# Attention rounds of a transformer kernel: the order of a pair's value products and the next pair's first transposes

## The chip, the cores and the metric

The kernel runs on one core of a Trainium2 chip, in one launch. The metric is the device time of one execution in microseconds (us). The median before the change is 3055.33 us, of two runs (3054.82 and 3055.84).

## The reference, cut to what matters

Two transformer layers and one recurrent and sparse-attention layer are computed for 512 tokens of width 1024, all in float32. Most of the work is matrix products; each kind of attention stands between an input projection and an output projection. What the change touches are the inner rounds of three attentions: layer 0 (`even_mixer`: 8 heads of banded attention with sinks, then 8 heads of stick-breaking attention), layer 1 (`odd_mixer`: 16 heads of dilated attention, computed here as one causal softmax with a table as bias) and the third layer (16 heads of attention over chosen keys).

```python
s = einsum('bnqhgd,bnkhd->bnhgqk', qb, kb) * (dh ** -0.5)
s = where(valid, s + bias, -inf)
p = exp(s - m);  denom = sum(p) (+ exp(sink - m))
o = einsum('bnhgqk,bnkhd->bnqhgd', p / denom, vb)
...
# stick breaking
a = where(strict, exp(log_sigmoid(z) + log_after), 0.0)
o = einsum('bhqk,bkhd->bqhd', a, v)
```

The order of the products is free as far as the reference goes.

## The kernel before, in words

All engine programs are written out by hand, one ordered list of instructions for each engine, with waits on named flags. There is no scheduler: the order in which the functions issue is the order on the engine.

**The three stages.** `Stage` (L1089) describes a run of rounds, one round for each pair of heads. `EV` (L2038) has eight rounds: four pairs of banded heads (`EA`, two groups of rows in a round: rows 2 and 3, rows 1 and 0) and four pairs of stick-breaking heads (`EB`, three groups: row 3, rows 2 and 0, row 1). `OC` (L2158) and `SX` (L2537) have eight rounds each, all with the three groups. Names in the trace begin with `ev`, `oc` and `sx`. A "row" i is a tile of 128 queries against the keys that it may see, so row 3 of a causal pair is 128x512. `u` is the head within the pair.

**A round on TensorE** is written in `pe_stage` (L1165), in the loop of L1246. For the pair g:
- `turn(g, 0, first group)` transposes the first group of head 0's weights (L1201; transposes are at L97). It waits until the bank is drained and until the row is scaled (`normed`, L1209).
- `scores(g + 1, n)` makes the scores of the next pair (L1181), in three places of the round, or two where the next pair has two groups.
- `fill(g, part)` issues matrix products of the projections that stand ahead of or behind the attention (L1169). The number in a round is the stage's `quota`; a table splits it over five places.
- the other `turn`s transpose the remaining groups of head 0 and those of head 1; the last group of head 1 comes just ahead of `fill(g, 3)` or `fill(g, 4)`.
- `values(g)` multiplies the transposed weights with the values (L1215). It waits until every transposed group of the pair has been copied out of PSUM.

Transposes and values share a ring of two PSUM banks (`tbank` and `vbank`, L1129 to L1133). The place in the ring is worked out from the pair and the group alone. The first transposes of pair g + 1 take the bank that the last transposes of pair g held, and the values of g take the other.

**A round on ScalarE** is in `act_stage` (L1273, loop at L1324): `upper(g - 1)` rounds the output of the pair before (it waits for `valued`), then the copy of the first transposed group, `exps(g, 1)`, the other copies with the splitting of projection weights between them (`act_split`), and at the end `copies(g, 1, last)` and then `exps(g + 1, 0)`: the exponentials of head 0 of the next pair. For stick-breaking pairs `sigmoids(g + 1, n)` take the place of the exponentials.

**A round on VectorE** is in `dve_stage` (L1363, loop at L1425): `end(g, 0)`, `lower(g - 1)`, the maxima of group 0 of the next pair, `end(g, 1)`, the other maxima, the weight splitting. `end` is `divide` (L1386: it waits for the exponentials of that head, takes the reciprocals, and scales row 3 first, then rows 2, 0 and 1, each giving `normed`) or `breaks` (L1400: a scan and a product for each row, after GpSimd's masks). `lower(g - 1)` waits for the values of the pair before and for ScalarE's upper half, and frees their bank.

The loop on TensorE before the change:

```python
for g in range(T_.N):
    turn(g, 0, slice(0, 1))
    scores(g + 1, 0)
    fill(g, 0)
    ...
    fill(g, 4)
    values(g)
```

Of the kernel before, what the change touches and what calls it, by code (L numbers as in the profile page):

```python
# [267 lines left out]
def program(nc, T, out):  # L268
# [109 lines left out]
    def handover(e, key):  # L378

        leave(e, key)  # L380
        if e.name != "pe":
            enter(e, key)
# [782 lines left out]
    def pe_stage(pe, T_, before, after, hand):  # L1165
        tag = T_.tag
        count = [0]

        def fill(g, part):  # L1169

            n = T_.quota[g]

            share = (0, 0.16, 0.5, 0.68, 0.86, 1) if g == T_.N - 1 else (0, 0.2, 0.4, 0.6, 0.8, 1)
            if T_.causal and 0 <= g < T_.N - 1:

                share = (0, 0.15, 0.35, 0.55, 0.7, 1)
            for _ in range(int(n * share[part + 1] + 1e-6) - int(n * share[part] + 1e-6)):
                next(before if count[0] < 96 else after)
                count[0] += 1

        def scores(g, n):  # L1181
            if g == T_.N or n >= len(T_.seq[g][0].groups):
                return
            A, s = T_.seq[g]
            kb = A.kv_of(s)
            pe.wait_ge(put, A.qkey(s))
            pe.wait_ge(put, A.kkey(kb))
            group = A.groups[n]
            for u in range(2):
                b = T_.sbanks[u]  # L1190
                pe.wait_ge(drained, pe.held[b])
                pe.held[b] = (tag, g, "s", n, u)
            for both in zip(T_.scores(g, n, 0), T_.scores(g, n, 1)):
                for u, (i, W, dst) in enumerate(both):
                    k0, k1, _, _ = A.spans[i]
                    r = slice(64 * u, 64 * u + 64)
                    ins = pe.matmul(dst, A.qT[r, s, i * P:(i + 1) * P], A.kT[r, kb, k0 * P:k1 * P], start=True, stop=True)
                    if i == group[-1]:
                        ins.then_inc(scored, (tag, g, n, u))

        def turn(g, u, part):  # L1201
            A, _ = T_.seq[g]
            for n in range(len(A.groups))[part]:
                group = A.groups[n]
                b, at = T_.tbank(g, u, n), 0
                pe.wait_ge(drained, pe.held[b])
                pe.held[b] = (tag, g, "t", n, u)
                for i in group:
                    pe.wait_ge(normed, (tag, g, u, i))  # L1209
                    for j in range(A.spans[i][3] // P):  # L1210
                        ins = pe.transpose(bank[b][:, at:at + P], T_.row(g, u, i)[:, j * P:(j + 1) * P], ident)
                        at += P
                ins.then_inc(turned, (tag, g, n, u))

        def values(g):  # L1215
            A, s = T_.seq[g]
            v = T_.vbank(g)
            o_ = bank[v]
            pe.wait_ge(drained, pe.held[v])
            pe.held[v] = (tag, "o", g)  # L1220
            for key in A.vkeys(s):
                pe.wait_ge(put, key)
            for u in range(2):
                for n in range(len(A.groups)):
                    pe.wait_ge(put, (tag, g, n, u))
            if A.total == CAUSAL_W:
                for kt in range(NT):
                    for u in range(2):
                        ins = pe.matmul(o_[64 * u:64 * u + 64, kt * P:S], A.V(2 * s + u, kt), T_.pt[u][:, kt, kt * P:S],
                                        start=kt == 0, stop=kt == NT - 1)  # L1230
            else:
                for i, (k0, k1, o, W) in enumerate(A.spans):
                    for kt in range(k0, k1):
                        for u in range(2):
                            ins = pe.matmul(o_[64 * u:64 * u + 64, i * P:(i + 1) * P], A.V(2 * s + u, kt),
                                            T_.pt[u][:, kt, i * P:(i + 1) * P], start=kt == k0, stop=kt == k1 - 1)
            ins.then_inc(valued, (tag, g))

        for _ in range(96 * T_.last):
            next(before)  # L1240
        for n in range(3):
            scores(0, n)
            fill(-1, n)
        fill(-1, 3)
        fill(-1, 4)
        for g in range(T_.N):  # L1246
            turn(g, 0, slice(0, 1))
            scores(g + 1, 0)
            fill(g, 0)
            turn(g, 0, slice(1, None))  # L1250
            fill(g, 1)
            scores(g + 1, 1)
            if g + 1 < T_.N:
                turn(g, 1, slice(0, -1))
                fill(g, 2)
            else:
                turn(g, 1, slice(0, 1))
                fill(g, 2)
                turn(g, 1, slice(1, -1))
            scores(g + 1, 2)  # L1260
            if g + 1 == T_.N or len(T_.seq[g + 1][0].groups) == 3:
                fill(g, 3)
                turn(g, 1, slice(-1, None))
            else:
                turn(g, 1, slice(-1, None))
                fill(g, 3)
            fill(g, 4)
            values(g)
        handover(pe, hand)
        for _ in after:  # L1270
            pass
# [1853 lines left out]
    def pe_program(pe):  # L3125
        pe.held = {}
        for l, C in enumerate(crosses):
            f1, f2 = ffns[f"f1{l}"], ffns[f"f2{l}"]
            if l:
                handover(pe, f1.up)  # L3130
                pe_gemm(pe, f1.up, {"h": hT(f1.up)}, rates_side(pe_rates, pe, f1.up))
            else:
                pe_f1u0(pe)
            pe_gemm(pe, f1.down, {"f": f1.F})
            handover(pe, "odd" if l else "even")
            pe_stage(pe, OC if l else EV, (pe_in1 if l else pe_in0)(pe), pe_out(pe, C), C.kv)
            pe_kv(pe, C)
            pe_xq(pe, C)
            pe_cross(pe, C)
            pe_gemm(pe, f"xo{l}", {"h": hT(f"xo{l}")})  # L3140
            handover(pe, f2.up)
            pe_gemm(pe, f2.up, {"h": hT(f2.up)}, rates_side(pe_rates, pe, f2.up))
            pe_gemm(pe, f2.down, {"f": f2.F})
# [3 lines left out]
        pe_rnn(pe)  # L3147
        pe_ya(pe)
        pe_stage(pe, SX, pe_products(pe, "gb", {"h": hT("idx2")}), pe_products(pe, "yb", {"h": hT("yb")}), "yb")
        pe_gemm(pe, "wo", {"y": Z})  # L3150
        pe_post(pe)
# [196 lines left out]
```

## Time and profile before

| | |
|---|---|
| median of two runs | 3055.33 us |
| the profiled execution | 3054.1 us |
| its span in the trace | 3052.4 us (1.7 us lie around it) |
| TensorE busy | 3037.4 us of the span |
| VectorE, ScalarE, GpSimd busy | 2036.1, 1416.4, 450.5 us |
| granted TensorE clock over the span | 0.999 of full |
| the rounds of EV, OC, SX in the span | about 447 to 537, 1555 to 1648, 2524 to 2617 us |

Times in timelines are counted from the span's start. Matmuls overlap, and their ends are modelled, so the time of a step on TensorE is best read from the start of one line to the start of the next.

### The profile page before, as it was taken

To read this page: it belongs to the slowest core of one execution; us is meant where nothing else is said; L and a number is where in the kernel's file an instruction comes from. 1 tells how busy PE (TensorE), PEld (TensorE's weight loads), DVE (VectorE), ACT (ScalarE), POOL (GpSimd) and SP (SyncE) were. 2 spreads that over 40 slices of the span, in tenths; PEclk is the share of its full clock that TensorE was granted. 3 is DMA by queue.
4 is the path that set the end of the run, shared out by engine and by line. 5 is a ranking of instruction groups with operands and counts; after the bars stand their busy time and mean duration, and the time that the engine had idled before them with its cause. 6 is when DMAs were issued, how large, how long until landed. Compare 5 with 4: busy or idle time off the path is not lost.

```text
span 3052.4 us, 44801 instructions
## 1 busy us (share of the span) xinstructions
PE 3037.4 (100%) x17960; PEld 2620.2 (86%) x17960; DVE 2036.1 (67%) x2896; ACT 1416.4 (46%) x2189; POOL 450.5 (15%) x550
## 2 busy tenths in 40 slices
PE   9999999999999999999999999999999999999999
PEld 8998886887999899988867879998887786789987
DVE  7886258755888478863565657886336876578873
ACT  5444247544444244442455545444236727454442
POOL 1112014212110021100310212110153200031100
PEclk9999999999999999999999999999999999999999
DMA  7762330423874267633232416763332231247732
GB/s 209 176 165 98 103 97 29 148 67 99 198 176 136 97 160 176 166 107 104 83 99 75 152 49 165 177 167 106 89 96 83 82 105 35 76 111 190 170 117 70
DMA packets 287360, 366.93 MB, mean 120 GB/s; under 512 B 12304, under 2 KB 211344, under 8 KB 287024
## 3 DMA queue, kind: packets, MB, share of 16 engines
q1 hardware_dynamic: 233392, 304.42, 31.5%
q0 software_dynamic: 53184, 59.32, 12.0%
q8 instruction: 142, 2.33, 0.3%
q14 instruction: 66, 0.54, 0.1%
q10 hardware_dynamic: 576, 0.33, 0.0%
HBM read 361.92 MB, written 2.10 MB: 119 GB/s over the span
## 4 chain that ended last, share of the span: by engine, by line
PE 94%; issue 3%; DVE 2%; POOL 1%; ACT 0%; DMA 0%; POOLq 0%; ACTq 0%; DVEq 0%
PE ps L94 91%; PE ps L97 3%; POOL evQ L142 1%; DVE wl L103 0%; POOL evPb L142 0%; POOL evPa L142 0%; DVE hTl L109 0%; DMA misc<-in_misc 0%; DVE xT L103 0%; DVE u_X2l L103 0%; DVE u_raw L103 0%; DVE u_X3l L103 0%; DVE u_X4l L103 0%; DVE evQ L115 0%; DVE s_gb L103 0%
## 5 line engine op out<-in xcount | busy, mean ns | idle before, releaser
L103 DVE TENSOR_TENSOR wl<-raw,wh 128x1024 fp32r<-128x1024 f32 (+2 forms) x485 | 597.0, 1237 | 499.1 <-ACT wh L100 494.9
L100 ACT ACTIVATE wh<-raw 128x1024 fp32r<-128x1024 f32 (+2 forms) x485 | 505.1, 1049 | 810.9 <-PE ps L94 770.0
L94 PE MATMUL ps<-hTh,wh 128*128 128x256 f32 (+1 forms) x2016 | 671.0, 333 | 0.7 <-ACT hTh L100 0.7
L94 PE MATMUL ps<-hTh,wl 128*128 128x256 f32 (+1 forms) x2016 | 666.6, 331 | 0.0
L94 PE MATMUL ps<-hTl,wh 128*128 128x256 f32 (+1 forms) x2016 | 624.0, 330 | 0.2 <-DVE hTl L109 0.2
L94 PEld LDWEIGHTS ps<-hTh,wh 128*128 128x128 f32 x2016 | 383.9, 190 | 42.1 <-issue 9.2
L94 PEld LDWEIGHTS ps<-hTh,wl 128*128 128x128 f32 x2016 | 383.7, 190 | 37.7 <-issue 7.1
L94 PEld LDWEIGHTS ps<-hTl,wh 128*128 128x128 f32 x2016 | 382.1, 190 | 37.4 <-issue 4.7
L100 ACT ACTIVATE wh<-u_raw 128x1024 fp32r<-128x1024 f32 x190 | 201.4, 1062 | 297.8 <-PE ps L94 281.9
L94 PE MATMUL ps<-u_Fh,wl 128*128 128x512 f32 x704 | 273.9, 389 | 0.0
L94 PE MATMUL ps<-u_Fh,wh 128*128 128x512 f32 x704 | 273.9, 389 | 0.0
L103 DVE TENSOR_TENSOR wl<-u_raw,wh 128x1024 fp32r<-128x1024 f32 x190 | 232.2, 1222 | 40.1 <-ACT wh L100 39.7
L103 POOL TENSOR_TENSOR xn<-xn 128x512 f32<-128x512 f32 x69 | 100.1, 1450 | 988.8 <-ACT xn L100 751.4
L94 PE MATMUL ps<-u_Fl,wh 128*128 128x512 f32 x704 | 232.9, 389 | 0.0
L94 PE MATMUL ps<-wh,hTh 128*128 128x512 f32 (+2 forms) x576 | 216.8, 377 | 0.0
L94 PE MATMUL ps<-wl,hTh 128*128 128x512 f32 (+2 forms) x576 | 215.1, 374 | 0.0
L94 PE MATMUL ps<-wh,hTl 128*128 128x512 f32 (+2 forms) x576 | 195.1, 374 | 0.0
L94 PEld LDWEIGHTS ps<-u_Fl,wh 128*128 128x128 f32 x704 | 132.1, 188 | 27.5
L94 PEld LDWEIGHTS ps<-u_Fh,wl 128*128 128x128 f32 x704 | 132.2, 188 | 27.3
L94 PEld LDWEIGHTS ps<-u_Fh,wh 128*128 128x128 f32 x704 | 132.1, 188 | 27.3
L94 PEld LDWEIGHTS ps<-wh,hTh 128*128 128x128 f32 x576 | 108.3, 188 | 20.1 <-issue 2.2
L94 PEld LDWEIGHTS ps<-wl,hTh 128*128 128x128 f32 x576 | 108.4, 188 | 19.2 <-issue 1.4
(423 smaller groups left out, 6106.6 us busy)
## 6 DMA issues: line engine op xcount, KB each, us to landing
raw<-in_ffn_w_gu SPq DMA_DIRECT2D x118, 512.0 KB, 4.6
raw<-in_ffn_w_down SPq DMA_DIRECT2D x88, 512.0 KB, 3.6
u_raw<-in_ffn_w_gu SPq DMA_DIRECT2D x77, 512.0 KB, 4.9
raw<-in_ffn_w_gu POOLq DMA_DIRECT2D x40, 512.0 KB, 6.1
u_raw<-in_ffn_w_gu POOLq DMA_DIRECT2D x38, 512.0 KB, 6.1
raw<-in_xa_w_kv SPq DMA_DIRECT2D x32, 512.0 KB, 3.6
raw<-in_w_in SPq DMA_DIRECT2D x28, 512.0 KB, 3.6
raw<-in_od_w_in SPq DMA_DIRECT2D x24, 512.0 KB, 3.8
```

Of the source, the lines that this page charges most:

```text
L94: return self.made(lambda e: e.matmul(*a, **k))
L97: return self.made(lambda e: e.transpose(*a, **k))
L100: return self.made(lambda e: e.activation(*a, **k))
L103: return self.made(lambda e: e.tensor_tensor(*a, **k))
L142: return self.made(lambda e: e.affine_select(*a, **k))
```

## The change

The call that issues the first transposes of head 0 moves from the top of the round to the end of the round before, ahead of `values`. Round 0 keeps its own at the top. The same instructions are issued with the same operands and banks; no other engine's program is touched.

```diff
@@ -1244,7 +1244,8 @@
         fill(-1, 3)
         fill(-1, 4)
         for g in range(T_.N):
-            turn(g, 0, slice(0, 1))
+            if not g:
+                turn(g, 0, slice(0, 1))
             scores(g + 1, 0)
             fill(g, 0)
             turn(g, 0, slice(1, None))
@@ -1265,6 +1266,8 @@
                 turn(g, 1, slice(-1, None))
                 fill(g, 3)
             fill(g, 4)
+            if g + 1 < T_.N:
+                turn(g + 1, 0, slice(0, 1))
             values(g)
         handover(pe, hand)
         for _ in after:
```

## Rows read from the trace of the kernel before

**Rows 1.** The page: busy time by engine, and the chain that ended last.
```profile
PE 3037.4 (100%) x17960; PEld 2620.2 (86%) x17960; DVE 2036.1 (67%) x2896; ACT 1416.4 (46%) x2189; POOL 450.5 (15%) x550
...
PE 94%; issue 3%; DVE 2%; POOL 1%; ACT 0%; DMA 0%; POOLq 0%; ACTq 0%; DVEq 0%
```

**Rows 2.** Timeline of TensorE, one round of OC (start, us, instruction, count).
```profile
1571.76 0.65 PE L97 MATMUL ps<-misc,ocPa 128*128 128x128 f32 x4
...
1574.98 0.38 PE L97 MATMUL ps<-misc,ocPb 128*128 128x128 f32 x2
...
1576.44 2.38 PE L94 MATMUL ps<-ocPT,o_v 128*64 128x512 f32 x16
1578.75 0.66 PE L97 MATMUL ps<-misc,ocPa 128*128 128x128 f32 x4
1579.33 1.13 PE L94 MATMUL ps<-o_kT,o_qT 64*128 64x512 f32 x4
```

**Rows 3.** Timeline of ScalarE, the same round (in brackets: idle before, releaser).
```profile
1575.39 0.38 ACT L100 ACTIVATE ocPT<-ps 128x256 f32<-128x256 f32 x1 [1.79 <-PE ps L97]
1575.67 0.39 ACT L100 ACTIVATE ocPb<-ocPb,ocsm 128x128 f32<-128x128 f32 x1
...
1578.86 0.60 ACT L100 ACTIVATE hTh<-ps 128x512 fp32r<-128x512 f32 x1 [0.90 <-PE ps L94]
```

**Rows 4.** Timeline of VectorE, the same round.
```profile
1570.75 0.49 DVE L106 TENSOR_SCALAR ocPa<-ocPa,ocsm 128x512 f32<-128x512 f32 x1
...
1577.99 0.18 DVE L124 RECIPROCAL ocsm<-ocsm 128x4 f32<-128x4 f32 x1 [1.43 <-ACT ocPa L100]
1578.20 0.49 DVE L106 TENSOR_SCALAR ocPa<-ocPa,ocsm 128x512 f32<-128x512 f32 x1
...
1579.56 0.69 DVE L103 TENSOR_TENSOR hTl<-ps,hTh 128x512 fp32r<-128x512 f32 x1
```

**Rows 5.** Timelines of TensorE and VectorE, a late round of OC.
```profile
1623.65 2.37 PE L94 MATMUL ps<-ocPT,o_v 128*64 128x512 f32 x16
...
1625.16 0.49 DVE L106 TENSOR_SCALAR ocPa<-ocPa,ocsm 128x512 f32<-128x512 f32 x1
```

**Rows 6.** Timelines of TensorE and VectorE, an early round of SX.
```profile
2545.34 2.37 PE L94 MATMUL ps<-sxPT,s_v 128*64 128x512 f32 x16
...
2547.10 0.49 DVE L106 TENSOR_SCALAR sxPa<-sxPa,sxsm 128x512 f32<-128x512 f32 x1
```

**Rows 7.** Timelines of TensorE and VectorE, first and third banded round of EV.
```profile
456.10 1.75 PE L94 MATMUL ps<-evPT,e_tk 128*64 128x128 f32 x28
...
457.16 0.36 DVE L106 TENSOR_SCALAR evPb<-evPb,evsm 128x256 f32<-128x256 f32 x1
...
477.55 1.75 PE L94 MATMUL ps<-evPT,e_tk 128*64 128x128 f32 x28
...
479.05 0.35 DVE L106 TENSOR_SCALAR evPb<-evPb,evsm 128x256 f32<-128x256 f32 x1
```

**Rows 8.** Timelines of TensorE and VectorE, a stick-breaking round of EV.
```profile
502.84 2.38 PE L94 MATMUL ps<-evPT,e_vb 128*64 128x512 f32 x16
...
501.06 0.69 DVE L103 TENSOR_TENSOR evPa<-evPa,evQ 128x512 f32<-128x512 f32 x1
...
505.96 0.69 DVE L103 TENSOR_TENSOR hTl<-ps,hTh 128x512 fp32r<-128x512 f32 x1
```

**Rows 9.** Waits of TensorE: in total us, times, longest us.
```profile
PE ps L94 <- ACT evQ L100: 3.7, 3, 2.2
```

**Rows 10.** Stretches of EV: length, each engine's busy us, granted clock, DMA.
```profile
482.60:484.86 2.26, 0.09 (x2) 0.04 (x1) 0.29 (x2) 2.26 (x7) 0.63 (x3) 1.00 0.00 0
484.86:486.20 1.34, 1.34 (x8) 0.92 (x8) 0.01 (x1) 1.23 (x3) 0.46 (x2) 0.75 0.00 0
486.20:488.00 1.80, 1.80 (x8) 1.57 (x7) 1.80 (x2) 1.72 (x5) 0.67 (x1) 0.50 0.00 0
488.00:489.00 1.00, 1.00 (x4) 0.41 (x4) 0.97 (x2) 1.00 (x4) 1.00 (x2) 0.53 0.61 35
```

## The prediction

> **What bounds the kernel now.** I read the page first, then TensorE's waits, then the timelines of TensorE, ScalarE and VectorE over the same round. The page shows TensorE busy for 3037.4 of 3052.4 us and on 94% of the chain that ended last [rows 1]. So a microsecond in which TensorE stands still is a microsecond of the kernel, and one on another engine costs nothing until TensorE has to wait for it. The longest kind of wait inside the rounds is 3.7 us in three pieces [rows 9], in the stick-breaking rounds. In OC and SX TensorE waits for nothing that counts. What the change does must therefore be read from one question: when TensorE reaches the moved transposes at their new place, is their input there?
>
> **Softmax rounds of three groups (OC and SX).** Follow the end of a round of OC. TensorE issues the last transposes of head 1 at 1574.98, then some filling products, the values at 1576.44, the first transposes of the next pair at 1578.75 and its scores at 1579.33 [rows 2]. ScalarE had waited 1.79 us for those last transposes; it copies them at 1575.39 and only then begins the next pair's exponentials, at 1575.67 [rows 3]. They take until VectorE, after 1.43 us of idling for them, starts the reciprocal at 1577.99; the 128x512 row is scaled from 1578.20 for 0.49, so it is there at 1578.69 [rows 4]. TensorE takes it at 1578.75. The values (2.31 us from start to start) are the cover of this chain, to within 0.06 us.
>
> The change takes the cover away. After the filling products TensorE reaches the moved transposes at 1576.44 and stands until 1578.69: 2.25 us. The values then queue behind the waiting transposes although their own input is there, and behind them everything on TensorE: the scores, the filling, the next transposes. Nothing of the chain can begin earlier in exchange, because it starts with ScalarE's copy of transposes that stand ahead of the wait, and from that copy to the scaled row it takes the same 3.3 us as before. So the wait isn't earned back in the next round, where the chain starts from a transposition that is as late as the round is.
>
> There are seven such boundaries in each stage (the round 0 transposes are not moved). The first four of OC show 2.24 to 2.25 us in this way. In the last three there is one filling product more, and the row is scaled at 1625.65 against values at 1623.65: 2.00 us [rows 5]. Sum 4 x 2.25 + 3 x 2.0 = 15.0 us. SX shows the same pattern at its seven (2547.59 against 2545.34 is 2.25 us [rows 6], the last three 2.0): 15.0 us.
>
> **Banded rounds (EV, pairs 0 to 3).** The first group begins with row 2. It is scaled at 457.52, the values began at 456.10: 1.42 us; the second boundary is the same; at the third VectorE first drains projection results, and the row comes at 479.40 against 477.55: 1.85 us [rows 7]. Sum 4.7 us.
>
> **Stick-breaking rounds (EV, four boundaries from pair 3 to 7).** Here the input is early: the product that makes row 3 ends at 501.75 and the values begin at 502.84 [rows 8]. The transposes pass without a wait. What is late next is the other side: the values end about 0.6 us later (the transposes take 0.58, 1578.75 to 1579.33 [rows 2]), and ScalarE's upper half (0.60 [rows 3]) and VectorE's lower half wait for them. The lower half, at 505.96 [rows 8], would start near 506.4, and VectorE's scans are queued behind it. VectorE and GpSimd are near their limit in these rounds. Ends: nothing, if their small gaps take it up, or the 0.45 us in each of four. I take 0.25 each, 1.0 us.
>
> **The same shift in the softmax rounds.** ScalarE's upper half starts 0.5 us later with regard to the scores. Head 1's row 3 is ready at 1571.24 and TensorE wants it at 1571.76 [rows 2, 4]: 0.52 us of room. It just goes; ends 0 and 0.1 us in each of 14 rounds, I take 0.
>
> **Handing over.** A row that TensorE now stands for costs the time from VectorE's end to its first transposition as well. I take the 0.06 us seen between 1578.69 and 1578.75 [rows 2, 4], for 17 boundaries 1.0 us. The filling products, copies, buffers and DMAs keep their order; the bank of the moved transposes is drained by the very copy that the values need, so no new wait stands there.
>
> Sum of the waits: 15.0 + 15.0 + 4.7 + 1.0 + 1.0 = 36.7 us.
>
> **The clock.** In EV there is a wait like the new ones: TensorE did nothing for some 2.2 us of 482.60 to 484.86. The granted clock was 1.00 through it and then 0.75, 0.50 (which is the 1.2 GHz level) and 0.53 in the next three stretches [rows 10]. What was lost is 0.25 x 1.34 + 0.5 x 1.80 + 0.47 x 1.00 = 1.7 us. The change makes 17 waits, 14 of them of 2.0 to 2.3 us and three of 1.4 to 1.9. One row can't say whether each such wait brings the clock down: the fall came after the wait, not in it, so how the wait lies seems to matter. Ends: no fall (0 us) and one at each (29 us). The nearest row fell, but three of the waits are clearly shorter and six more a little. I take half of them, 8 x 1.7 = 13.6 us.
>
> In the Trainium skill, "TensorE: Matmul & The Clock Gate", section "HAM oscillation — how this bites in real kernels", a kernel is described whose wait in every tile brought the clock down every time. By that each of the 17 waits would pay; it is the second rival below. This trace agrees for its one long wait, 2.2 us followed by a clock of 0.50, and can't show the repetition.
>
> **Total.** 36.7 + 13.6 = 50.3 us on the profiled execution's 3054.1 us: 3104.4. The median lies 1.2 us above that execution, so I say 3105 us, 1.6% slower. A measurement of this kernel can tell about 2% (61 us) from no change, so the forecast lies inside that bound.
>
> **Rivals.**
> 1. The waits come, the clock stays up, or falls two or three times only. For: at most one fall happened before, and between the waits TensorE is fully busy. Against: the one wait of this length was followed by a fall. 3055.3 + 36.7 = 3092, up to 3097.
> 2. The clock falls after nearly every wait: 3055.3 + 36.7 + 17 x 1.7 = 3121. If it falls after the 14 long ones, 3116. For: the row named. Against: the shorter waits, and that a fall needs the wait to lie badly.
> 3. Not slower. The mechanism would be that the first transposes use time in which TensorE has nothing else. That needs the scaled row before the values begin. It decides at that point: in the stick-breaking rounds it holds by 1.1 us, in all 17 others it fails by 1.4 to 2.25 us [rows 4 to 8]. If ScalarE made the exponentials ahead of the last copy, or much faster, the change would be free everywhere, and what could be won is the waits of the rounds, at most the 3.7 us of [rows 9]: 3052 to 3055. The program orders say otherwise.
> 4. The transposes don't wait as I read it, because the values are let past them. The median would be unchanged, 3055. Nothing in the timelines shows matmuls out of program order.
>
> **How the numbers follow.** The forecast (about half the falls, 3099 to 3113) gets 0.50; rival 1 0.22; rival 2 0.20; rivals 3 and 4 together 0.04; the rest, 0.04, is for a loss that I don't see, such as a late second head in all rounds (14 x 0.1 us and more). The range that leaves out two in ten reaches from the clean sum with a microsecond or two less to rival 2's end: 3088 to 3121. Slower by over 2% means above 3116.4: most of rival 2's upper half and a bit of the rest, 0.11. Faster by over 2% has no mechanism: 0.01. Within 2%: 0.88.
>
> **What would show it.** The waits of TensorE should list VectorE's scaled rows (ocPa, sxPa, evPb, L106) as new releasers, seven times each for OC and SX with about 2.0 to 2.3 us, three times for the banded pairs with 1.4 to 1.9, and none for the stick-breaking pairs. A round of OC should grow by 2.0 to 2.3 us at full clock, and its stretches should show a granted clock below 1 in about half of the rounds. VectorE's and ScalarE's busy times should not move. I am wrong if TensorE's new idle time in OC is far from 15 us, if the stages' growth is not the sum of waits and low-clock losses, or if the time outside the three stages changes.

## The result, and the profile after

The changed kernel takes 3109.88 us (two runs, 3107.5 and 3112.26) against 3055.33: ratio 1.0179, 95% interval 1.0163 to 1.0196. It is slower by 54.6 us, 1.8%, which is more than any spread of either kernel. The forecast was 3105.

The page of the changed kernel, its first lines and the chain that ended last, answers to [rows 1]:

```profile
span 3105.7 us, 44801 instructions
...
PE 3050.4 (98%) x17960; PEld 2624.2 (84%) x17960; DVE 2035.0 (66%) x2896; ACT 1413.8 (46%) x2189; POOL 451.1 (15%) x550
...
PE 90%; DVE 3%; issue 3%; ACT 3%; POOL 0%; POOLq 0%; DVEq 0%; ACTq 0%
```

The instructions are the same in number, and VectorE and ScalarE are busy for as long as before. TensorE's busy time rose by 13 us (3050.4 against 3037.4) with the same work, and its idle time by 40 (3105.7 - 3050.4 = 55.3 against 15.0). Two readings follow: where it idles, and why the same products take longer.

TensorE's waits after the change (total us, times, longest), beside [rows 9]:

```profile
PE ps L97 <- DVE ocPa L106: 15.5, 7, 2.3
PE ps L97 <- DVE sxPa L106: 15.5, 7, 2.3
PE ps L97 <- DVE evPb L106: 5.2, 3, 2.2
PE ps L94 <- ACT evQ L100: 3.8, 3, 2.3
PE ps L94 <- DVE ocsm L112: 1.7, 6, 0.4
PE ps L94 <- DVE sxsm L112: 1.3, 5, 0.4
```

The first three lines are the 17 waits that were forecast, for the rows that VectorE scales. The last two are new and were not forecast.

The timeline of TensorE over one round of OC, start to start, beside [rows 2]:

```profile
1573.72 0.63 PE L97 MATMUL ps<-misc,ocPa 128*128 128x128 f32 x4 [2.32 <-DVE ocPa L106]
1574.28 2.37 PE L94 MATMUL ps<-ocPT,o_v 128*64 128x512 f32 x16
1576.59 1.13 PE L94 MATMUL ps<-o_kT,o_qT 64*128 64x512 f32 x4
...
1580.84 0.63 PE L97 MATMUL ps<-misc,ocPa 128*128 128x128 f32 x4
...
1583.00 0.70 PE L94 MATMUL ps<-o_kT,o_qT 64*128 64x256 f32 x4 [0.40 <-DVE ocsm L112]
...
1588.29 0.63 PE L97 MATMUL ps<-misc,ocPa 128*128 128x128 f32 x4 [2.32 <-DVE ocPa L106]
...
1588.85 4.07 PE L94 MATMUL ps<-ocPT,o_v 128*64 128x512 f32 x16
1592.85 1.13 PE L94 MATMUL ps<-o_kT,o_qT 64*128 64x512 f32 x4
```

The transposes now stand for 2.32 us, the values behind them. In the middle of the round a score product waits 0.40 us for a bank. The values took 2.31 us from start to start at 1574.28, but 4.00 at 1588.85. The stretches of these values and of those two boundaries later (length, busy by engine, granted clock, DMA) say why:

```profile
1574.28:1576.59 2.31, 2.31 (x18) 1.07 (x17) 0.09 (x1) 0.00 (x0) 0.00 (x0) 1.00 0.25 95
1588.85:1592.85 4.00, 4.00 (x18) 1.61 (x17) 0.08 (x1) 0.00 (x0) 0.00 (x0) 0.57 0.23 85
1605.11:1607.41 2.30, 2.30 (x17) 1.06 (x16) 0.08 (x1) 0.00 (x0) 0.00 (x0) 1.00 0.00 0
1619.67:1623.67 4.00, 4.00 (x17) 1.56 (x16) 0.09 (x1) 0.00 (x0) 0.00 (x0) 0.57 0.22 81
```

After every second wait of OC the clock fell, to its 1.2 GHz level for most of the values, which cost 4.00 - 2.31 = 1.7 us. In the profiled run that happened at three boundaries of OC, three of SX and one of EV. The profiled run is the faster of the two, 3107.5 us at a mean granted clock of 0.996. The other took 3112.26 at 0.994 and has no trace. The clock share of the first, 0.004 x 3106 = 12 us, fits its seven falls; 0.006 x 3110 = 19 us in the second gives an estimate of ten or eleven.

The view of the transposes by what they read (count, min/median/max ns, first and last start) gives the growth of each stage. Before:

```profile
L97 PE MATMUL ps<-misc,evPb x88: 270/272/473, 447.1 to 537.0; 128*128 128x128 f32 x88
L97 PE MATMUL ps<-misc,o_t x64: 270/272/273, 1461.3 to 1533.5; 128*128 128x128 f32 x64
L97 PE MATMUL ps<-misc,s_tq x64: 270/272/273, 2250.8 to 2312.7; 128*128 128x128 f32 x64
L97 PE MATMUL ps<-misc,sxPa x64: 270/273/330, 2524.3 to 2611.5; 128*128 128x128 f32 x64
L97 PE MATMUL ps<-misc,c0t x48: 270/272/332, 607.5 to 665.7; 128*128 128x128 f32 x48
L97 PE MATMUL ps<-misc,c1t x48: 270/273/332, 1715.8 to 1774.0; 128*128 128x128 f32 x48
```

After:

```profile
L97 PE MATMUL ps<-misc,evPb x88: 270/272/330, 447.0 to 543.6; 128*128 128x128 f32 x88
L97 PE MATMUL ps<-misc,o_t x64: 270/272/273, 1467.9 to 1540.2; 128*128 128x128 f32 x64
L97 PE MATMUL ps<-misc,s_tq x64: 270/273/273, 2281.2 to 2343.0; 128*128 128x128 f32 x64
L97 PE MATMUL ps<-misc,sxPa x64: 270/273/329, 2554.7 to 2664.9; 128*128 128x128 f32 x64
L97 PE MATMUL ps<-misc,c0t x48: 270/272/328, 614.1 to 672.3; 128*128 128x128 f32 x48
L97 PE MATMUL ps<-misc,c1t x48: 270/273/329, 1746.1 to 1804.4; 128*128 128x128 f32 x48
```

EV, from the first evPb to the first c0t: 160.4 to 167.1, +6.7. OC, from the first o_t to the first c1t: 254.5 to 278.2, +23.7. SX, from the first s_tq to the last sxPa: 360.7 to 383.7, +23.0. Together 53.4 us of a span that grew by 53.3, so the time outside the three stages did not change. These three distances serve as the measure in what follows. OC's is 15.5 of waits and 3 x 1.7 = 5.1 of low clock, which leaves 3.1; SX's leaves 2.4. The experiments were made to take these parts away one by one.

### The profile page after: what moved, and what is told of

Read it like the earlier page. It is cut to its first block, busy times and chain, and to the rows that moved or that the text cites. A ratio compares the mean times of both kernels' runs of the same rounds, so it can differ in the third digit from the quotient of the medians.

```text
span 3105.7 us, 44801 instructions
## 1 busy us (share of the span) xinstructions
PE 3050.4 (98%) x17960; PEld 2624.2 (84%) x17960; DVE 2035.0 (66%) x2896; ACT 1413.8 (46%) x2189; POOL 451.1 (15%) x550
## 4 chain that ended last, share of the span: by engine, by line
PE 90%; DVE 3%; issue 3%; ACT 3%; POOL 0%; POOLq 0%; DVEq 0%; ACTq 0%
PE ps L94 88%; PE ps L97 2%; ACT sxPb L100 1%; ACT ocPb L100 1%; DVE wl L103 0%; ACT sxPa L100 0%; ACT ocPa L100 0%; ACT hTh L100 0%; DVE evQ L115 0%; DVE ocPb L112 0%; DVE sxPb L112 0%; DVE ocPa L106 0%; DVE sxPa L106 0%; ACT sxPT L100 0%; ACT ocPT L100 0%
## 5 line engine op out<-in xcount | busy, mean ns | idle before, releaser
L94 PEld LDWEIGHTS ps<-hTh,wl 128*128 128x128 f32 x2016 | 383.7, 190 | 38.3 <-issue 7.8
```

Source lines behind the costliest of these rows:

```text
L94: return self.made(lambda e: e.matmul(*a, **k))
```

## The experiments

All ran beside the kernel before: 3054.98 us in the first group of four (15 runs), 3054.88 in the second (13 runs). Apart from the order of TensorE's or ScalarE's instructions they compute the same.

**The stages one by one.** The condition for the move becomes the following; the two `return` lines belong to one kernel each.

```diff
+        def moved(g):
+            return 0 < g < T_.N and T_.causal          # only OC and SX
+            return 0 < g < T_.N and T_.seq[g][0].stick # the other kernel
...
-            if not g:
+            if not moved(g):
                 turn(g, 0, slice(0, 1))
...
-            if g + 1 < T_.N:
+            if moved(g + 1):
                 turn(g + 1, 0, slice(0, 1))
```

> Moves the first transposes only in OC and SX; EV keeps the old order. My account (each boundary pays its own wait): the first stage gives back its growth of 6.8 us, so about 3103 us, ratio near 1.0156, and the OC and SX waits for the scaled rows stay at 15.5 us each. Rival (the loss is a general one, such as one longer program or other code): the time stays near 3110.

Measured: 3104.36 us (four runs), ratio 1.0161, 1.0147 to 1.0175. The waits stay at 15.5 and 15.5. EV's distance goes back to 160.9, OC grew by 23.6, and SX by 25.4. SX had four falls of the clock in the profiled run instead of three, 1.7 us; the median misses 3103 by 1.4. The loss belongs to the stages, and each pays its own.

> Moves the first transposes only ahead of the four stick-breaking pairs, where the row is ready before the values begin. My account: no wait for the row, only the shift of the pair before's output by 0.6 us; within 2 us of the kernel before, 3055 to 3057. Rival (the values pay for anything put in front of them): 4 x 0.6 us of delay or more, 3058 and up; rival on the other side (the move as such is a gain where the row is ready): under 3054.

Measured: 3055.14 us (eleven runs), ratio 1.0001, 0.9992 to 1.0010. Where the row is ready first, the move neither costs nor gains anything that eleven runs can tell; both rivals fall. One thing is not equal in the two traces: EV of the kernel before has a fall of the clock, and this one has none. It is worth little there. EV's distance is 160.4 before and 160.3 here, and kernels of this study that keep the old order in EV read 160.9 and 160.4 with the fall, 159.9 without it.

**Work in the waits.** Ahead of the moved transposes, TensorE turns the identity into the bank of the values:

```diff
+        def busy(g, n):
+            v = T_.vbank(g)
+            pe.wait_ge(drained, pe.held[v])
+            for _ in range(n):
+                pe.transpose(bank[v][:, 0:P], ident, ident)
...
             if g + 1 < T_.N:
+                busy(g, 0 if T_.seq[g + 1][0].stick else 14 if T_.causal else 9)
                 turn(g + 1, 0, slice(0, 1))
```

> As the changed kernel, but TensorE fills each of the 17 waits with transposes of the identity into the bank that the values overwrite next (14 of them in OC and SX, about 1.9 us; 9 in banded rounds, about 1.2 us). They are extra work inside a wait. Theory of the clock (six more falls cost 6 x 1.7 us): no fall in OC and SX and about 3100 us. Rival (the low clock is a by-product that costs nothing, or the remaining gap is enough for a fall): 3110. If the waits were not pure waits, 17 x 1.9 us would be added: 3140.

Measured: 3098.43 us (four runs), ratio 1.0142, 1.0128 to 1.0156: 11.5 us faster than the changed kernel (8.1 by the two profiled runs, 3099.41 against 3107.5) with 223 more transposes. Its timeline at one boundary of OC, then its waits:

```profile
1601.45 1.69 PE L97 MATMUL ps<-misc 128*128 128x128 f32 x14
1603.93 0.63 PE L97 MATMUL ps<-misc,ocPa 128*128 128x128 f32 x4 [0.79 <-DVE ocPa L106]
```

```profile
PE ps L97 <- DVE sxPa L106: 4.8, 7, 0.8
PE ps L97 <- DVE ocPa L106: 4.8, 7, 0.8
...
PE ps L97 <- DVE evPb L106: 2.3, 3, 1.2
PE ps L94 <- DVE ocsm L112: 1.7, 6, 0.4
PE ps L94 <- DVE sxsm L112: 1.7, 6, 0.4
```

The extra work is free, so the waits are pure waits. The clock of both stages reads 1.00 throughout:

```profile
1563.00:1669.10 106.10, 99.01 (x606) 65.33 (x604) 59.42 (x215) 64.02 (x195) 5.39 (x10) 1.00 0.16 50
2550.80:2656.80 106.00, 98.91 (x605) 65.30 (x604) 59.25 (x215) 63.80 (x195) 0.00 (x0) 1.00 0.08 26
```

OC and SX grew by 18.8 us each instead of 23.7 and 23.0. Keeping TensorE at work through the wait keeps the clock, and the six falls were worth 4.9 + 4.2 = 9.1 us, close to 6 x 1.7. EV gained nothing (+6.8); its clock fell once all the same, for twice as long, behind a wait that was there before.

**The late second head.** On ScalarE, the exponentials of head 1 go ahead of the output of the pair before:

```diff
+            early = g >= 1 and not turning(g) and T_.causal
+            if early:
+                exps(g, 1)
             if g >= 1:
                 upper(g - 1)
...
-            if not turning(g):
+            if not turning(g) and not early:
                 exps(g, 1)
```

> As the changed kernel, but in OC and SX ScalarE makes the exponentials of head 1 ahead of the output of the pair before, while it idles for the values. Theory: the 0.3 to 0.5 us in each full-clock round (waits for ocsm and sxsm, 3.0 us in the list, 5.5 us by the stages' growth) come from ScalarE starting head 1 later with regard to the scores; they go, and the time is 3104 to 3105. Rival (they come from the transposes' weight loads after a wait or from VectorE's lower half): 3109 or more. The waits for the scaled rows stay at 15.5 us each.

Measured: 3096.82 us (four runs), ratio 1.0137, 1.0123 to 1.0150. The waits for the scaled rows are still 15.5 and 15.5, and those for ocsm and sxsm are gone from the list. OC and SX grew by 17.8 each. The gain is larger than expected because the clock fell only once in each stage instead of three times; that part (4 x 1.7 = 6.8 us) was not forecast. To tell the two apart, both edits were joined:

> Both earlier edits together: identity transposes in the waits, and the exponentials of head 1 early. Without falls in OC and SX and without the late score banks the two stages should grow by the waits alone, about 16 us each, and EV by 6.8: 3055 + 32 + 7 = 3094 us, with at most one fall less or more. Rival (the gains of the two edits are the same microseconds): 3097 to 3098, no better than each alone.

Measured: 3092.96 us (four runs), ratio 1.0124, 1.0109 to 1.0139. The two stages grew by 16.2 and 16.1. With no fall in either kernel, the step from the busy waits alone (18.8) to both (16.15) is the price of the late second head: 2.65 us in each stage. With head 1 early in both, the step from 17.8 (one fall) to 16.15 is the price of one fall: 1.65 us. In OC and SX the kernel before has no fall and waits neither for ocsm nor for sxsm, so early exponentials had no such wait to win there. The rival, that both edits win the same microseconds, falls.

**The dose.** If a boundary pays for lost cover, cover given back must come off the bill. First, one of the four key tiles of the values ahead of the moved transposes:

```diff
+            values(g, 0 if T_.causal else None)
             if g + 1 < T_.N:
                 turn(g + 1, 0, slice(0, 1))
-            values(g)
+            if T_.causal:
+                values(g, 1)
```

> As the changed kernel, but in OC and SX the first key tile of the values (512 of their 1280 columns, some 0.9 us of 2.31) is issued ahead of the moved transposes, the rest behind. Theory (a boundary pays what stands between TensorE's arrival and the scaled row): the 14 waits shrink from 2.0 to 2.3 us to about 1.1 to 1.4, 13 us less, and at that length they bring no fall of the clock: about 3087 us. If the clock falls as before: 3097. Rival (the cost is the order as such, whatever the cover): 3107 or more.

Measured: 3079.43 us (four runs), ratio 1.0081, 1.0064 to 1.0098. The edit does more than its expectation says: in EV it issues all values first, which is the old order, and EV's distance is back at 159.9. With EV's 6.7 us taken off, the expectation is 3080. At a boundary of OC:

```profile
1578.09 1.08 PE L94 MATMUL ps<-ocPT,o_v 128*64 128x512 f32 x4
1580.38 0.66 PE L97 MATMUL ps<-misc,ocPa 128*128 128x128 f32 x4 [1.22 <-DVE ocPa L106]
1580.97 1.52 PE L94 MATMUL ps<-ocPT,o_v 128*64 128x384 f32 x12
```

The wait shrank from 2.32 to 1.22, the total from 15.5 to 7.8 in each stage, the clock never fell, and OC and SX grew by 12.3 each. That is 6.5 less than with the busy waits (18.8, no fall either), while the waits are 7.7 us shorter than the changed kernel's 15.5. Some of the difference is in the steps themselves: from the start of the first values to the next scores the boundary shown takes 4.32 us (1578.09 to 1582.41), against 2.89 before (1576.44 to 1579.33 in [rows 2]). That is 1.43 more, with a listed wait of 1.22.

Second, filling products moved into the gap, in the kernel with early exponentials and, as a control, in the kernel before:

```diff
-                share = (0, 0.15, 0.35, 0.55, 0.7, 1)
+                share = (0, 0.15, 0.3, 0.45, 0.55, 1)
```

> As the kernel with early exponentials, but in OC and SX two or three filling products of each round are moved from between the earlier steps to between the last transposes and the moved ones (8 instead of 5 or 6 there). 36 products of 0.23 us in all stand in front of the waits that were behind them: if the chain from the last copy to the scaled row keeps its 3.3 us, the waits shrink by 8 us, the falls with them, and the time is 3085 to 3088. Rival (the steps that lose the filling wait for score banks or scaled rows instead): the scaled-row waits shrink by 8 us, new ones take their place, 3095 or more.

> The kernel before with the same shift of filling products. There the values cover the chain already, so nothing is to be won: 3055 if the earlier steps have room, and 3056 to 3063 if they begin to wait. The excess over 3055 is the price that the shift has by itself in the run beside it.

Measured: 3087.66 us (four runs), ratio 1.0106, 1.0091 to 1.0121, and for the control 3058.63 (ten runs), ratio 1.0012, 1.0003 to 1.0021. In the first, the waits for scaled rows shrank from 15.5 to 9.8 in each stage, and one wait of 1.9 or 1.8 us for a projection result on ScalarE took the place of the seventh. No clock fell, and the stages grew by 13.3 and 13.2. Of the 4.5 us that each gained on the kernel with early exponentials (17.8), 1.65 is its one fall. The control pays 3.7 us for new waits on score banks (1.6 us in each stage by the list) and wins nothing, because there the values cover the chain already. The same edit is a gain of 9 us in one order and a loss of 4 in the other. About 4.6 of the 9 us are clock and not cover: the two falls of OC and SX, 3.3, and 1.3 in EV, which the edit does not touch but where the clock did not fall this time (165.5 against 166.8).

## Why the prediction was right, and where it was not

**The mechanism held.** The cover of 2.31 us was what the chain from the last copy to the scaled row had to itself. The waits were forecast at 15.0 + 15.0 + 4.7 and 1.0 for handing over, 35.7 us, and measured 15.5 + 15.5 + 5.2 = 36.2. Most of the excess is at the third banded boundary, 2.23 us instead of 1.85. The time for handing over was put too low: where TensorE stands for a row, it goes 0.14 to 0.15 us after VectorE's end (1573.58 to 1573.72), not 0.06. Nothing was earned back in the next round. The kernel with one key tile ahead, the one with late filling and the control show that it is the cover, not the order as such.

**The stick-breaking pairs** were put at 1.0 us. The kernel that moves only there can't be told from the kernel before (0.2 us, interval from 0.9992 to 1.0010). The lower end was right.

**The clock** was put at eight falls of 1.7 us, 13.6 us. The size of a fall was right in OC and SX (1.65 to 1.7). The profiled run has six falls there, 10 us, and one in EV, where the kernel before has one too, which the forecast had not taken off. By the estimate above the other run had three or four more, so half of the 17 boundaries is close to the mean of the two; the number itself was a guess between the ends. The edit that keeps TensorE at work in the wait shows the cause. Rival 1 (none, or two or three) and rival 2 (nearly all) both fall: the clock fell at 7 of the 17.

A fall does not always cost its 1.7 us. In the changed kernel EV's fall follows the new wait at 482.85, and from there to the next wait for evQ, at 491.57, it is 8.72 us; with the late filling, which has the same order in EV and no fall, it is 7.11 (483.58 to 490.69): 1.6 us paid. In the kernel before, the fall stands ahead of scores that at full clock would have waited: the kernel that moves only the stick-breaking pairs has no fall there, and its list shows a wait of 1.06 us for evQ in its place. And one of SX's three falls reached into the round behind it, where no score product then waited for its bank: sxsm is listed five times, not six.

The Trainium skill, "TensorE: Matmul & The Clock Gate", section "HAM oscillation — how this bites in real kernels", tells of a kernel whose clock fell in every tile. That did not happen here: in this trace it fell at every second boundary of OC. The waits of the kernel told there are, by the page, DMA waits of some 3 to 5 us, longer than any of the 17, so the prediction leaned on it too far when it said that by it each would pay.

**The step that failed** is "The same shift in the softmax rounds": "It just goes; ends 0 and 0.1 us in each of 14 rounds, I take 0." It measured 2.65 us in each of the two stages, 5.3 us together, nearly 0.4 us in each round. I had looked at head 1's row 3 alone, with 0.52 us of room against a shift of 0.5. Even there 0.11 us were lost in each such round: the transposes of ocPa start 4.25 us after the pair's first scores (1580.84 - 1576.59), against 4.14 (1571.76 - 1567.62), because the handing over of 0.15 us needs room as well. The larger part is further on. The same late exponentials hold up VectorE's next maxima, which stand behind head 1's scaling in its program, and the maxima free the score bank. ScalarE and VectorE in the round shown above, beside [rows 3, 4]:

```profile
1576.70 0.60 ACT L100 ACTIVATE hTh<-ps 128x512 fp32r<-128x512 f32 x1 [3.86 <-PE ps L94]
```

```profile
1577.40 0.69 DVE L103 TENSOR_TENSOR hTl<-ps,hTh 128x512 fp32r<-128x512 f32 x1 [3.04 <-ACT hTh L100]
...
1580.20 0.49 DVE L106 TENSOR_SCALAR ocPa<-ocPa,ocsm 128x512 f32<-128x512 f32 x1
1580.61 0.87 DVE L106 TENSOR_SCALAR ocPb<-ocPb,ocsm 128x384 f32<-128x384 f32 x3
1581.39 0.55 DVE L112 CUSTOM_DVE_ANT_0 ocPb<-ps,o_t 128x384 f32<-128x384 f32 x1
...
1582.56 0.28 DVE L112 CUSTOM_DVE_ANT_0 ocPb<-ps,o_t 128x128 f32<-128x128 f32 x1
```

ScalarE stands idle for 3.86 us and only then begins; the last maximum of that group ends at 1582.84, and TensorE's scores, which wanted the bank at 1582.60, begin at 1583.00. The same three moments before the change (TensorE, VectorE, TensorE), and the two of TensorE in the kernel with both edits:

```profile
1567.62 1.13 PE L94 MATMUL ps<-o_kT,o_qT 64*128 64x512 f32 x4
1573.10 0.29 DVE L112 CUSTOM_DVE_ANT_0 ocPb<-ps,o_t 128x128 f32<-128x128 f32 x1
1573.54 0.70 PE L94 MATMUL ps<-o_kT,o_qT 64*128 64x256 f32 x4
```

```profile
1576.87 1.13 PE L94 MATMUL ps<-o_kT,o_qT 64*128 64x512 f32 x4
1582.73 0.70 PE L94 MATMUL ps<-o_kT,o_qT 64*128 64x256 f32 x4
```

Counted from the pair's first scores, the last of these maxima ended at 1573.10 + 0.29 - 1567.62 = 5.77 us before the change and 1582.84 - 1576.59 = 6.25 after. The scores that need the bank began at 5.92 and at 6.41, so 0.15 and 0.16 us behind it: before the change there was no room left at all, and the whole shift of 0.48 went into the round. With head 1 early they begin at 5.86. In the three rounds ahead of the last three boundaries of each stage, where one more filling product stands ahead of these scores (they begin at 6.09 or 6.10 before), the shift costs 0.3 us and shows as a wait of 0.17. Some 0.2 us of the 2.65 are thus not the late head's, but what the early exponentials win over the kernel before (5.86 against 5.92 in three rounds).

The sum then reads 36.2 of waits, 10.2 of low clock and 5.3 of late second heads, 51.7 of 53.4 us. The remaining 1.7 is the balance of small terms that the traces show. On the one side, a boundary costs 0.06 us more than its listed wait (from the last filling product it is 1588.29 - 1585.59 = 2.70 us, against 0.32 to the values before: 2.38, not 2.32); each stage's last round has a new wait of 0.38 us; and EV's fall costs 1.6 us instead of at most some 0.5. On the other side stands the part of SX's fall that hid a wait. The profiled run was forecast at 3104.4 us and took 3107.5. That it was hit to 3 us owes something to errors of opposite sign: the clock term was 3.4 too high and the stick-breaking term 1.0, the shift term 5.3 too low and the rest 2.2. The median is 4.9 off; the difference is the other run, which had more falls by the estimate.

Rival 3 named the point from which the order would cost nothing, the row ready before the values. It holds for the stick-breaking pairs, where no cost could be measured, and nowhere else. No kernel of this study beats the one before.

## What to carry to other kernels

A block of work that waits for nothing may be the cover of a chain on other engines: before moving an instruction ahead of it, look up when the instruction's own input is complete and compare that with the block's start, not with its end. When a block is delayed, follow everything that is released by its end through the program order of each engine, down to the buffers that those instructions free; the tightest slack need not be at the first consumer (here it was 0.5 us there, and none at the score bank), and a hand-over needs some of it (0.15 us here). And price a wait of about 2 us on TensorE higher than its length: here the clock fell behind 7 of 17, and most falls cost another 1.7 us.

## What the runs showed of the hardware

- Equal waits don't all bring the clock down. In OC of the changed kernel four waits of 2.3 us were followed, in turn, by values of 2.31, 4.00, 2.30 and 4.00 us. In the kernel with early exponentials the same 14 waits of 2.0 to 2.3 us were followed by two falls instead of six. The old 2.17 us wait of EV brought one in the kernel before and none in the kernel that moves only the stick-breaking pairs, where it has the same length.
- Shorter waits brought none: 1.2 us and less in OC and SX of the kernel with one key tile ahead, and 1.9 us and less there with the late filling.
- The falls lost 1.7 us of clock each. One, in EV of the kernel with the busy waits, lost twice that (0.30 x 1 + 0.50 x 6 + 0.11 x 1 = 3.4 us):

```profile
490.00:491.00 1.00, 0.12 (x2) 0.15 (x2) 0.00 (x0) 1.00 (x4) 0.58 (x3) 0.70 0.00 0
491.00:497.00 6.00, 5.98 (x20) 3.72 (x21) 4.51 (x5) 4.34 (x13) 3.34 (x7) 0.50 0.25 87
497.00:498.00 1.00, 1.00 (x7) 0.82 (x6) 0.83 (x3) 0.85 (x4) 1.00 (x4) 0.89 0.00 0
```

  What decides whether and for how long it falls was not settled.
- Transposes of the identity, 14 of them (1.69 us) in each wait, writing a bank that nobody reads before it is overwritten, were enough to keep the clock at its upper level: it read 1.00 over all of OC and SX, in both kernels that have them.
